# Convolution layers: the pivot subtracted by TensorE in the tap bank, sums two tiles later, GpSimd's copies issued ahead of the sigmoid

## The chip, the cores and the metric

One core of a Trainium2 chip runs the whole program in one launch. TensorE (PE; its weight loads PEld), VectorE (DVE), ScalarE (ACT), GpSimd (POOL) and SyncE (SP, which issues the loads) each run their own list of instructions in order and wait for each other by semaphores. The metric is the device time of the program in microseconds, the median of three runs.

## The reference

A transformer block of four mixers and then four layers, for 512 tokens of width 1024 in float32. Layers 0 and 3 of the four have the convolution module that is changed here:

```
def dwconv(x, w, b):
    k, c = w.shape
    y = lax.conv_general_dilated(
        x, w[:, None, :].astype(x.dtype), window_strides=(1,),
        padding=[(k // 2, k // 2)], dimension_numbers=('NWC', 'WIO', 'NWC'),
        feature_group_count=c)
    return y + b

def conv_module(h, w_in, b_in, dw_w, dw_b, ln_g, ln_b, w_out):
    a, gt = jnp.split(h @ w_in + b_in, 2, axis=-1)
    u = a * jax.nn.sigmoid(gt)
    u = dwconv(u, dw_w, dw_b)
    u = layernorm(u, ln_g, ln_b)
    return jax.nn.silu(u) @ w_out
```

The convolution has 31 taps per channel (CONV_WIDTH). The layer norm takes the mean over 1024 channels and the mean of the squared differences from it.

## The kernel before, in words

Activations lie transposed: 8 chunks of 128 channels by 512 tokens. A linear layer goes output block by output block; a block of `conv_in` has 8 weight tiles of 128 x 128. A tile (`mac`, lines 1391 to 1393) is three passes of TensorE with 512 columns: weights and activations are split into a high and a low part of type float32r (XH, XL, WH, WL; HH and HL for hidden activations), and three of the four products are added up. Weights come as float32 (RAW) 8 tiles at a time; ScalarE makes the high part (line 1642), GpSimd the low part (line 2367).

In `conv_layer` blocks 2c and 2c + 1 of `conv_in` belong to chunk c: the even one is the gate half, the odd one the value half. `evac` is called behind each block. For an even block VectorE scales it out of its bank (line 1951, the "even scaling") and ScalarE takes the sigmoid (line 1723). For an odd block VectorE scales and multiplies by the gate (line 2196), which gives u in a padded buffer PD. Then the 31 taps of the chunk are shared: the first TAPS_PE[c] go to TensorE, as float32 matmuls with diagonal matrices (line 1569), which ScalarE makes (line 1838); the next TAPS_POOL[c] are copied with their gain by ScalarE (`pool_tap`, lines 1847 and 1845) into seven staging slots in BI and added by GpSimd (line 2385); VectorE has the rest (`dve_taps`), in two halves: the first half behind the gating of its own chunk, the second behind that of the next one. VectorE's first, third, ... tap gather in one bank, its second, fourth, ... in TensorE's tap bank, so its second tap waits for TensorE's taps. Two joins (lines 2226 and 2228) add up the three parts.

For the layer norm every chunk's output has a pivot subtracted, the mean over the 128 channels of chunk 0: TensorE's `pivot` (line 1583), ScalarE's copy out of the bank (line 1857). Chunks 0 and 1 have it subtracted later (`less_pivot`, line 2246), the others in VectorE's first tap (line 2208; without a pivot lines 2205 and 2214). Then ScalarE squares a chunk (line 1671) and TensorE adds up the chunk and its square over channels in two banks (`add_up`, line 1577).

The order on each engine is that in which `walk` calls the steps. Work that isn't due yet is put in two queues: `later(fn, delay, first=True)` in `soon`, sorted by the tile at which it is due, and without `first` in `bg`; behind each tile one due step is taken, from `soon` first. PSUM has 8 banks, handed out in turn (`banks`); a bank that is taken again waits for what last freed it.

At the end of the layer VectorE finishes chunk 7 (`join_last`), its square and sums follow, `keep_warm(n)` puts n matmuls of no use on TensorE, and mean, scale and SiLU lead to the output projection `conv_out`.

Of the kernel before, what the change touches and what calls it, by code (L numbers as in the profile page):

```python
# [9 lines left out]
T = 512  # L10
# [15 lines left out]
OUT_ORDER = (4, 5, 0, 1, 2, 3, 6, 7)  # L26
TAPS_PE = (2, 3, 3, 4, 4, 4, 6, 16)
TAPS_POOL = (8, 8, 8, 8, 8, 8, 8, 7)
# [113 lines left out]
def build(nc, wst, xin, prm, cst, gatew, cmpw1, cmpw2, relm, natb, rope, dist, out):  # L142
# [7 lines left out]
    with ExitStack() as ctx:  # L150
# [81 lines left out]
        def walk(steps):  # L232
# [708 lines left out]
            def conv_layer(norm, nxt, ci, bias_free):  # L941
                cur = {}
# [5 lines left out]
                def tap(c, j):  # L948
                    return pcol("conv_dw_w", 248 * ci + 31 * c + j)
# [17 lines left out]
                def dve_taps(ch, a, b):  # L967
                    c = ch["c"]
                    j0 = TAPS_PE[c] + TAPS_POOL[c]
                    step("dve_taps", ci, c, a, b, ch["own"].ap, ch["own"].free, ch["two"].ap, ch["two"].free, ch["pe"],  # L970
                         ch["pad"].ap[:, j0:542], [tap(c, j) for j in range(j0, 31)], cur["p"].ap if c > 1 else None, cur["p_made"] if c > 1 else None,
                         ch["u"])

                def finish(ch):
# [16 lines left out]
                    if c == 0:  # L991
                        later(pivot, 13, first=True)
                        return
                    if c == 1:
                        for k in range(2):
                            o, made = outs[k]
                            outs[k] = (o, (step("less_pivot", o.ap, cur["p"].ap, made, cur["p_made"]), "o"))
                            later(lambda k=k: square(k), 13, first=True)
                            later(lambda k=k: add_up(k), 18)
                        cur["d"], cur["var"] = banks.get(), banks.get()  # L1000
                    elif c < 7:
                        later(lambda: square(c), 13, first=True)
                        later(lambda: add_up(c), 18)

                def pivot():
                    bank = banks.get()
                    cur["p"] = tiles.get()
                    i = step("pivot", cur["p"].ap, cur["p"].free, outs[0][0].ap, outs[0][1], bank.ap, bank.free)
                    bank.done((i, "p"))
                    cur["p_made"] = (i, "p")  # L1010

# [22 lines left out]
                def evac(m, bank, made):  # L1034
                    c = m // 2
                    n_pe = TAPS_PE[c]
                    if m % 2 == 0:
                        g = tiles.get()
                        z = scaled(g.ap, bank, norm, made, g.free)
                        i = step("sigmoid", g.ap, g.ap, pcol("conv_b_in", 16 * ci + 8 + c), (z,))  # L1040
                        cur["g"] = (g, (i, "sig"))
                        if c:
                            pool_taps(cur["ch"], TAPS_POOL[c - 1] // 2, TAPS_POOL[c - 1])
                        return
# [18 lines left out]
                    def pe_taps():  # L1063
                        step("pe_taps", dgs, dg_made, pad.ap, ch["u"], ch["acc"].ap, ch["acc"].free, ch["pe"])
                        for s in dg:
                            s.done(ch["pe"])
# [10 lines left out]
                step("tables")  # L1077
                keep_warm(2)
                finish(cur["ch"])
# [3 lines left out]
                keep_warm(4)  # L1083
                cur["p"].done(("tap", ci, 7, 0))
                pt_free[0] = pt_free[1] = (cur["squares"],)
# [297 lines left out]
        def tensor(e):  # L1383
# [178 lines left out]

            def pe_taps(i, dgs, dg_made, pad, u_made, bk, bk_free, event):
                for x in bk_free:
                    w.wait_ge(*at(x))
                w.wait_ge(*at(dg_made))
                w.wait_ge(*at(u_made))
                for j in range(len(dgs)):
                    t = e.matmul(bk, dgs[j], pad[:, j:j + T], start=j == 0, stop=j == len(dgs) - 1)  # L1569
                t.then_inc(*did(pe_made, event))  # L1570

            def add_up(i, first, last, d, d_free, o, o_made):
# [4 lines left out]
                e.matmul(d, ones, o, start=first, stop=last).then_inc(*did(pe_made, (i, "mm")))  # L1577

            def pivot(i, p, p_free, o, o_made, bank, bank_free):
                for event in bank_free:  # L1580
                    w.wait_ge(*at(event))
                w.wait_ge(*at(o_made))
                e.matmul(bank, ones, o, start=True, stop=True).then_inc(*did(pe_made, (i, "mm")))

# [28 lines left out]
            def ret_out(i, c, os, made, bank, bank_free, g, g_made, gain):  # L1613
# [10 lines left out]
                nat_scores=nat_scores, nat_turn=nat_turn, nat_values=nat_values, gates=gates, cmp_product=cmp_product, cmp_kv=cmp_kv, cmp_norm=cmp_norm, cmp_scores=cmp_scores,  # L1624
                cmp_turn=cmp_turn, cmp_values=cmp_values, pe_taps=pe_taps, add_up=add_up, pivot=pivot, warm=warm, ret_scores=ret_scores,
                ret_values=ret_values, ret_out=ret_out))

        def scalar(e):
# [223 lines left out]

            def pivot(i, p, p_free, o, o_made, bank, bank_free):
                for event in p_free:
                    w.wait_ge(*at(event))
# [57 lines left out]
        def vector(e):  # L1913
# [283 lines left out]

            def dve_taps(i, ci, c, a, b, own, own_free, two, two_free, pe_event, pad, taps, p, p_made, u_made):
# [407 lines left out]
```

## Time and profile before

| what | us |
|---|---|
| median of three runs | 3226.23 (3224.87 to 3229.0) |
| the profiled execution | 3229.4 |
| its span, first to last instruction | 3227.6 |
| TensorE busy in the span | 3151.7 (98%) |
| VectorE, ScalarE, GpSimd busy | 1451.8, 1255.6, 1545.0 |

The span is what the trace covers; the execution's own time is 1.8 us longer. Busy times are sums over instructions; a matmul's end is modelled, so starts are compared here rather than ends.

### The profile page before, as it was taken

What the parts mean: (1) busy time and instruction counts of PE and PEld (TensorE: products, weight loads), DVE (VectorE), ACT (ScalarE), POOL (GpSimd) and SP (SyncE); (2) the same over time, 40 slices, a digit from 0 to 9 for tenths busy, and PEclk for the clock granted to TensorE, in tenths of its full rate; (3) what the DMA queues carried; (4) which work ended last, traced back from release to release, by engine and by line L of the source; (5) the groups of instructions that cost most, each with busy time, mean ns of one, the idle gap of its engine ahead of it and who ended that gap; (6) DMA issues with size and microseconds to landing.
All of it is one profiled execution on the core that took longest, in us unless ns stands there. A gap on an engine that the chain in (4) does not pass through costs nothing. (4 is left out here: it accounts for less than half of the span.)

```text
span 3227.6 us, 34930 instructions
## 1 busy us (share of the span) xinstructions
PE 3151.7 (98%) x13893; PEld 2472.8 (77%) x13893; DVE 1451.8 (45%) x2674; ACT 1255.6 (39%) x1858; POOL 1545.0 (48%) x764
## 2 busy tenths in 40 slices
PE   8999999989999999999999999999999998999999
PEld 5668888865788887778888877787888885578887
DVE  5554111388643345446243523331624359853433
ACT  5553222255443345554343322222434344543333
POOL 3225555567354453334554533443455457545454
PEclk9999999999999999999999999999999999999999
DMA  4213333221232333222323322222232331133322
GB/s 182 76 46 92 98 92 98 92 68 56 66 99 97 98 98 102 94 86 87 103 92 98 112 70 67 72 91 68 90 104 92 98 98 53 40 92 101 95 96 88
DMA packets 80674, 286.03 MB, mean 89 GB/s; under 512 B 9088, under 2 KB 9344, under 8 KB 80384
## 3 DMA queue, kind: packets, MB, share of 16 engines
q1 hardware_dynamic: 80512, 283.80, 27.8%
q8 instruction: 110, 1.80, 0.2%
q14 instruction: 52, 0.43, 0.0%
HBM read 281.40 MB, written 2.10 MB: 88 GB/s over the span
## 5 line engine op out<-in xcount | busy, mean ns | idle before, releaser
L2367 POOL TENSOR_TENSOR WL<-RAW,WH 128x1024 fp32r<-128x1024 f32 x504 | 1216.8, 2416 | 1257.4 <-ACT WH L1642 1257.1
L1391 PE MATMUL PS<-XH,WH 128*128 128x512 f32 x2640 | 1076.4, 408 | 30.1 <-ACT TT L1857 14.0
L1393 PE MATMUL PS<-XH,WL 128*128 128x512 f32 x2640 | 1032.2, 391 | 0.0
L1392 PE MATMUL PS<-XL,WH 128*128 128x512 f32 x2640 | 1031.9, 391 | 0.0
L1642 ACT ACTIVATE WH<-RAW 128x1024 fp32r<-128x1024 f32 x504 | 529.2, 1051 | 548.1 <-PE PS L1393 458.8
L1391 PEld LDWEIGHTS PS<-XH,WH 128*128 128x128 f32 x2640 | 498.3, 189 | 171.4 <-issue 45.7
L1392 PEld LDWEIGHTS PS<-XL,WH 128*128 128x128 f32 x2640 | 498.5, 189 | 116.2 <-issue 19.0
L1393 PEld LDWEIGHTS PS<-XH,WL 128*128 128x128 f32 x2640 | 497.7, 189 | 105.8
L1391 PE MATMUL PS<-HH,WH 128*128 128x512 f32 x1264 | 495.6, 392 | 8.6 <-DVE HL L2265 4.4
L1392 PE MATMUL PS<-HL,WH 128*128 128x512 f32 x1264 | 493.5, 390 | 0.0
L1393 PE MATMUL PS<-HH,WL 128*128 128x512 f32 x1264 | 493.3, 390 | 0.0
L1946 DVE TENSOR_TENSOR X<-PS,X 128x512 f32<-128x512 f32 x168 | 115.2, 688 | 507.0 <-PE PS L1393 507.0
L2372 POOL TENSOR_TENSOR HL<-TT,HH 128x512 fp32r<-128x512 f32 x142 | 184.2, 1298 | 329.8 <-ACT HH L1646 329.6
L1951 DVE TENSOR_TENSOR PD<-PS,TT 128x512 f32<-128x512 f32 x178 | 123.3, 693 | 375.1 <-PE PS L1393 355.6
L1391 PEld LDWEIGHTS PS<-HH,WH 128*128 128x128 f32 x1264 | 238.3, 189 | 61.4 <-issue 6.1
L1393 PEld LDWEIGHTS PS<-HH,WL 128*128 128x128 f32 x1264 | 238.3, 189 | 49.8
L1392 PEld LDWEIGHTS PS<-HL,WH 128*128 128x128 f32 x1264 | 238.4, 189 | 49.4 <-issue 0.2
L1744 ACT ACTIVATE PS<-PD,PRM 128x512 f32<-128x512 f32 x176 | 137.8, 783 | 224.1 <-DVE PD L1951 223.7
L1646 ACT ACTIVATE HH<-TT 128x512 fp32r<-128x512 f32 x142 | 90.0, 634 | 340.5 <-DVE PD L1927 177.9
L2187 DVE SCALAR_TENSOR_TENSOR PS<-PD,PRM,PS 128x512 f32<-128x512 f32 x176 | 133.0, 756 | 149.9 <-ACT PS L1744 149.9
L1951 DVE TENSOR_TENSOR TT<-PS,TT 128x512 f32<-128x512 f32 x118 | 90.5, 767 | 240.2 <-PE PS L1393 222.5
L2219 DVE SCALAR_TENSOR_TENSOR PS<-PD,PRM,PS 128x512 f32<-128x512 f32 x268 | 179.1, 748 | 16.1 <-PE PS L1569 16.1
(242 smaller groups left out, 2414.5 us busy)
## 6 DMA issues: line engine op xcount, KB each, us to landing
RAW<-wst SPq DMA_DIRECT2D x504, 512.0 KB, 3.5
BI<-natb SPq DMA_DIRECT2D x16, 384.0 KB, 4.5
X<-xin SPq DMA_DIRECT2D x16, 256.0 KB, 5.0
X<-cmpw SPq DMA_DIRECT2D x1, 2048.0 KB, 9.5
out<-X SPq DMA_DIRECT2D x8, 256.0 KB, 2.0
BI<-relm SPq DMA_DIRECT2D x4, 448.0 KB, 10.4
PRM<-prm SPq DMA_DIRECT2D x1, 685.0 KB, 12.8
BI<-rope SPq DMA_DIRECT2D x2, 256.0 KB, 4.1
```

The source lines that it names most:

```text
L1391: e.matmul(o, wh, h, start=first, stop=False)
L1392: e.matmul(o, wh, l, start=False, stop=False)
L1393: t = e.matmul(o, wl, h, start=False, stop=last)
L1642: e.activation(WH[:, b % NSPLIT, :], RAW[:, b % NRAW, :], ACT.Copy).then_inc(*did(hi_made, ("hi", b)))
L1646: e.activation(HH[:, k, :], src, ACT.Copy).then_inc(*did(act_made, (i, "hi")))
L1744: e.activation(bank, pad[:, 1:513], ACT.Identity, scale=pcol("ffn_dw_w", 132 * layer + 44 + ch), bias=pcol("ffn_dw_b", 44 * layer + ch)).t ...
L1946: e.tensor_tensor(X[:, m, :], bank, X[:, m, :], ADD).then_inc(*did(dve_made, (i, "x")))
L1951: e.tensor_tensor(dst, bank, rs, MUL).then_inc(*did(dve_made, (i, "z")))
L2187: e.scalar_tensor_tensor(bank, pad[:, 0:512], pcol("ffn_dw_w", wn + ch), bank, MUL, ADD).then_inc(*did(dve_made, (i, "l")))
L2219: e.scalar_tensor_tensor(bank, pad[:, n:n + T], taps[n], bank, MUL, ADD).then_inc(*did(dve_made, ("tap", ci, c, n)))
L2367: e.tensor_tensor(WL[:, b % NSPLIT, :], RAW[:, b % NRAW, :], WH[:, b % NSPLIT, :].bitcast(f32), SUB).then_inc(*did(lo_made, ("lo", b)))
L2372: e.tensor_tensor(HL[:, k, :], src, HH[:, k, :].bitcast(f32), SUB).then_inc(*did(pool_made, (i, "lo")))
```

## The change

Five things are done in the convolution layers. (1) The pivot is no longer brought out of a bank: ScalarE writes −1/128 as a weight tile into HL and a copy of chunk 0's output into HH, both of type float32r, and TensorE multiplies the two: once into the bank of the sums (`pivot_sum`, where chunks 0 and 1 take it from, line 2241 of the new file) and once per chunk from chunk 2 on at the end of its tap matmuls. VectorE's first tap has the plain form in all chunks. The sum over chunks takes chunk 0 in. (2) Two taps of TensorE, one in chunk 4 and one in chunk 6, go to VectorE. (3) The sums are due 20 tiles behind their chunk's joins instead of 18, in the sorted queue; the banks of the sums are taken one chunk earlier. (4) The second half of a chunk's copies for GpSimd stands ahead of the next sigmoid. (5) Two of the six `keep_warm` matmuls go.

```
-TAPS_PE = (2, 3, 3, 4, 4, 4, 6, 16)
+TAPS_PE = (2, 3, 3, 4, 3, 4, 5, 16)
...
                     if c == 0:
                         later(pivot, 13, first=True)
+                        later(pivot_sum, 20, first=True)
+                        cur["d"], cur["var"] = banks.get(), banks.get()
                         return
                     if c == 1:
                         for k in range(2):
                             o, made = outs[k]
-                            outs[k] = (o, (step("less_pivot", o.ap, cur["p"].ap, made, cur["p_made"]), "o"))
+                            outs[k] = (o, (step("less_pivot", o.ap, cur["d"].ap, made, ("pivot_sum", ci)), "o"))
                             later(lambda k=k: square(k), 13, first=True)
-                            later(lambda k=k: add_up(k), 18)
-                        cur["d"], cur["var"] = banks.get(), banks.get()
+                            later(lambda k=k: add_up(k), 20, first=True)
                     elif c < 7:
                         later(lambda: square(c), 13, first=True)
-                        later(lambda: add_up(c), 18)
+                        later(lambda: add_up(c), 20, first=True)
...
                 def add_up(k):
                     o, made = outs[k]
-                    if k:
-                        i = step("add_up", k == 1, k == 7, cur["d"].ap, cur["d"].free, o.ap, made)
-                        cur["mean"] = (i, "mm")
+                    i = step("add_up", k == 0, k == 7, cur["d"].ap, (outs[0][1], outs[1][1]), o.ap, made)
+                    cur["mean"] = (i, "mm")
...
                     if m % 2 == 0:
+                        if c:
+                            pool_taps(cur["ch"], TAPS_POOL[c - 1] // 2, TAPS_POOL[c - 1])
                         g = tiles.get()
                         z = scaled(g.ap, bank, norm, made, g.free)
                         i = step("sigmoid", g.ap, g.ap, pcol("conv_b_in", 16 * ci + 8 + c), (z,))
                         cur["g"] = (g, (i, "sig"))
-                        if c:
-                            pool_taps(cur["ch"], TAPS_POOL[c - 1] // 2, TAPS_POOL[c - 1])
                         return
...
                 step("tables")
-                keep_warm(2)
                 finish(cur["ch"])
...
+            def pivot_sum(i, ci, d, d_free):
+                for event in d_free:
+                    w.wait_ge(*at(event))
+                w.wait_ge(*at(("pivot", ci)))
+                e.matmul(d, HL[:, 7, 0:128], HH[:, 7, :], start=True, stop=True).then_inc(*did(pe_made, ("pivot_sum", ci)))
+
...
                 for j in range(len(dgs)):
-                    t = e.matmul(bk, dgs[j], pad[:, j:j + T], start=j == 0, stop=j == len(dgs) - 1)
+                    t = e.matmul(bk, dgs[j], pad[:, j:j + T], start=j == 0, stop=pivot_made is None and j == len(dgs) - 1)
+                if pivot_made is not None:
+                    w.wait_ge(*at(pivot_made))
+                    t = e.matmul(bk, HL[:, 7, 0:128], HH[:, 7, :], start=False, stop=True)
...
-            def pivot(i, p, p_free, o, o_made, bank, bank_free):
-                for event in p_free:
-                    w.wait_ge(*at(event))
-                w.wait_ge(*at((i, "mm")))
-                e.activation(p, bank, ACT.Copy, scale=1.0 / 128).then_inc(*did(act_made, (i, "p")))
+            def pivot(i, event, o, o_made):
+                e.activation(HL[:, 7, 0:128], ones, ACT.Copy, scale=-1.0 / 128)
+                w.wait_ge(*at(o_made))
+                e.activation(HH[:, 7, :], o, ACT.Copy).then_inc(*did(act_made, event))
...
-                        if p is None:
-                            t = e.tensor_scalar(own, pad[:, 0:T], taps[0], None, MUL)
-                        else:
-                            w.wait_ge(*at(p_made))
-                            t = e.scalar_tensor_tensor(own, pad[:, 0:T], taps[0], p, MUL, SUB)
-                        t.then_inc(*did(dve_made, ("tap", ci, c, 0)))
+                        e.tensor_scalar(own, pad[:, 0:T], taps[0], None, MUL).then_inc(
+                            *did(dve_made, ("tap", ci, c, 0)))
...
-                e.tensor_tensor(o, o, p, SUB).then_inc(*did(dve_made, (i, "o")))
+                e.tensor_tensor(o, p, o, ADD).then_inc(*did(dve_made, (i, "o")))
```

ScalarE in chunk 1 and the start of chunk 2 of the first convolution layer, the difference in its order (WH is the weight split, line 1723 the sigmoid, lines 1847 and 1845 the copies for GpSimd):

```order
-L1723 ACTIVATE TT<-TT,PRM 128x512
-L1845 ACTIVATE BI<-PD,PRM 128x512 x4
-L1642 ACTIVATE WH<-RAW 128x1024
-L1857 ACTIVATE TT<-PS 128x512
+L1845 ACTIVATE BI<-PD,PRM 128x512 x4
+L1723 ACTIVATE TT<-TT,PRM 128x512
+L1642 ACTIVATE WH<-RAW 128x1024
+L1854 ACTIVATE HL<-CST 128x128
+L1856 ACTIVATE HH<-TT 128x512
 L1847 ACTIVATE BI<-PD,PRM 128x512
 L1845 ACTIVATE BI<-PD,PRM 128x512 x3
 L1838 ACTIVATE PT<-CST,PRM 128x128 x4
```

The sigmoid has moved behind the four copies, and two copies out of SBUF (lines 1854 and 1856 of the new file) stand where the copy out of the pivot's bank stood.

TensorE around the pivot in the same layer, before: the pivot's matmul behind the fifth tile of block 5, the rest of that block, and the first pass of block 6 (bank PS2):

```order
L1583 MATMUL PS2<-TT,CST 128x512 [waits dve_made]
L1391 MATMUL PS3<-XH,WH 128x512
L1392 MATMUL PS3<-XL,WH 128x512
L1393 MATMUL PS3<-XH,WL 128x512
L1391 MATMUL PS3<-XH,WH 128x512
L1392 MATMUL PS3<-XL,WH 128x512
L1393 MATMUL PS3<-XH,WL 128x512
L1391 MATMUL PS3<-XH,WH 128x512
L1392 MATMUL PS3<-XL,WH 128x512
L1393 MATMUL PS3<-XH,WL 128x512
L1391 MATMUL PS2<-XH,WH 128x512 [waits lo_made,act_made]
```

And now, in block 6: the fourth tile, the pivot's sum, the fifth tile, and chunk 2's taps:

```order
L1388 MATMUL PS2<-XH,WH 128x512
L1389 MATMUL PS2<-XL,WH 128x512
L1390 MATMUL PS2<-XH,WL 128x512
L1564 MATMUL PS1<-HH,HL 128x512 [waits act_made]
L1388 MATMUL PS2<-XH,WH 128x512
L1389 MATMUL PS2<-XL,WH 128x512
L1390 MATMUL PS2<-XH,WL 128x512
L1572 MATMUL PS5<-PD,PT 128x512 [waits dve_made]
L1572 MATMUL PS5<-PD,PT 128x512 x2
L1575 MATMUL PS5<-HH,HL 128x512
```

The matmul of 512 float32 columns in block 5 has gone; block 6 no longer waits for ScalarE, and a pass of HL and HH stands in block 6 and behind the taps. The first pass of block 6 is in bank PS2 as before and waits for VectorE, which scaled block 4 out of it.

TensorE at the sums of chunk 1 in block 8, before:

```order
L1577 MATMUL PS5<-TT,CST 128x512
L1577 MATMUL PS1<-TT,CST 128x512 [waits act_made]
L1391 MATMUL PS2<-XH,WH 128x512
L1392 MATMUL PS2<-XL,WH 128x512
L1393 MATMUL PS2<-XH,WL 128x512
L1391 MATMUL PS2<-XH,WH 128x512
L1392 MATMUL PS2<-XL,WH 128x512
L1393 MATMUL PS2<-XH,WL 128x512
L1569 MATMUL PS0<-PD,PT 128x512 [waits dve_made]
L1569 MATMUL PS0<-PD,PT 128x512 x3
```

And now, with those of chunk 0 (banks PS1 for the chunks, PS3 for the squares):

```order
L1583 MATMUL PS1<-TT,CST 128x512
L1583 MATMUL PS3<-TT,CST 128x512 [waits act_made]
L1388 MATMUL PS2<-XH,WH 128x512
L1389 MATMUL PS2<-XL,WH 128x512
L1390 MATMUL PS2<-XH,WL 128x512
L1583 MATMUL PS1<-TT,CST 128x512
L1583 MATMUL PS3<-TT,CST 128x512 [waits act_made]
L1388 MATMUL PS2<-XH,WH 128x512
L1389 MATMUL PS2<-XL,WH 128x512
L1390 MATMUL PS2<-XH,WL 128x512
L1572 MATMUL PS0<-PD,PT 128x512 [waits dve_made]
L1572 MATMUL PS0<-PD,PT 128x512 x3
```

The two pairs of sums stand behind the fourth and fifth tile of the block now, not around the third, and each pair has a sum of the chunk ahead of that of its square.

## Rows read from the trace of the kernel before

**Rows 1.** Busy times by stretch; columns: stretch, its length, then each engine, granted clock, DMA

```profile
666.66:821.11 154.45, 134.97 (x450) 86.18 (x449) 133.35 (x206) 79.20 (x140) 105.06 (x69) 0.96 0.16 51
...
2661.39:2814.65 153.26, 134.53 (x450) 86.14 (x448) 133.38 (x206) 79.21 (x140) 105.04 (x69) 0.96 0.16 51
```

**Rows 2.** Waits of TensorE, 640 to 840 us: total us, times, longest

```profile
PE PS L1577 <- ACT TT L1671: 7.1, 4, 3.0
...
PE PS L1391 <- ACT TT L1857: 6.9, 1, 6.9
```

**Rows 3.** TensorE in order of time: start us, us, instruction [idle before <-releaser]

```profile
698.20 0.80 PE L1391 MATMUL PS<-XH,WH 128*128 128x512 f32 x1 [6.89 <-ACT TT L1857]
...
706.07 0.40 PE L1392 MATMUL PS<-XL,WH 128*128 128x512 f32 x1
...
713.10 0.39 PE L1393 MATMUL PS<-XH,WL 128*128 128x512 f32 x1
```

**Rows 4.** ScalarE in order of time, chunks 1 to 3

```profile
693.55 0.72 ACT L1723 ACTIVATE TT<-TT,PRM 128x512 f32<-128x512 f32 x1 [9.83 <-DVE PD L1927]
...
694.18 2.54 ACT L1845 ACTIVATE BI<-PD,PRM 128x512 f32<-128x512 f32 x4
...
697.58 0.57 ACT L1857 ACTIVATE TT<-PS 128x512 f32<-128x512 f32 x1
...
718.58 1.14 ACT L1671 ACTIVATE TT<-TT 128x512 f32<-128x512 f32 x2
```

**Rows 5.** VectorE in order of time, chunks 1 to 3

```profile
692.84 0.68 DVE L1951 TENSOR_TENSOR TT<-PS,TT 128x512 f32<-128x512 f32 x1
...
694.38 0.75 DVE L2196 SCALAR_TENSOR_TENSOR PD<-PS,PRM,TT 128x512 f32<-128x512 f32 x1 [0.22 <-ACT TT L1723]
...
701.81 0.69 DVE L2226 TENSOR_TENSOR TT<-PS,BI 128x512 f32<-128x512 f32 x1
...
703.14 3.16 DVE L2246 TENSOR_TENSOR TT<-TT 128x512 f32<-128x512 f32 x2
...
707.92 6.01 DVE L2219 SCALAR_TENSOR_TENSOR PS<-PD,PRM,PS 128x512 f32<-128x512 f32 x9
...
713.85 0.67 DVE L1951 TENSOR_TENSOR TT<-PS,TT 128x512 f32<-128x512 f32 x1
...
730.63 2.07 DVE L2219 SCALAR_TENSOR_TENSOR PS<-PD,PRM,PS 128x512 f32<-128x512 f32 x3 [5.03 <-PE PS L1569]
```

**Rows 6.** Two short stretches with the granted clock (PEclk, third column from the right)

```profile
698.20:701.40 3.20, 3.20 (x8) 2.55 (x9) 3.20 (x6) 3.20 (x7) 3.06 (x3) 0.50 0.00 0
...
719.25:725.10 5.85, 5.85 (x10) 2.98 (x10) 5.73 (x9) 5.13 (x10) 5.65 (x4) 0.50 0.11 9
```

**Rows 7.** TensorE in order of time, end of the first layer

```profile
794.64 13.98 PE L1569 MATMUL PS<-PD,PT 128*128 128x512 f32 x32 [1.67 <-DVE PD L2196]
...
808.46 3.60 PE L1577 MATMUL PS<-TT,CST 128*128 128x512 f32 x8
...
813.60 1.88 PE L1577 MATMUL PS<-TT,CST 128*128 128x512 f32 x4
```

**Rows 8.** Groups of VectorE instructions by line, 655 to 821 us: busy us, mean ns

```profile
L2208 DVE SCALAR_TENSOR_TENSOR PS<-PD,PRM,TT 128x512 f32<-128x512 f32 x6 | 8.9, 1486 | 0.0
...
L2228 DVE TENSOR_TENSOR TT<-PS,TT 128x512 f32<-128x512 f32 x7 | 4.8, 692 | 0.2
...
L2246 DVE TENSOR_TENSOR TT<-TT 128x512 f32<-128x512 f32 x2 | 3.2, 1620 | 0.0
...
L2205 DVE TENSOR_SCALAR PS<-PD,PRM 128x512 f32<-128x512 f32 x2 | 1.5, 749 | 0.0
```

**Rows 9.** First weight wait of the output projection; VectorE in the second layer

```profile
835.18 0.47 PE L1391 MATMUL PS<-HH,WH 128*128 128x512 f32 x1 [1.35 <-POOL WL L2367]
...
2687.69 0.68 DVE L1951 TENSOR_TENSOR TT<-PS,TT 128x512 f32<-128x512 f32 x1
```

**Rows 10.** GpSimd in order of time, chunk 2

```profile
702.80 4.64 POOL L2385 TENSOR_TENSOR BI<-BI 128x512 f32<-128x512 f32 x3
```

More of the change, by code:

```diff
@@ L970, in dve_taps @@
                     step("dve_taps", ci, c, a, b, ch["own"].ap, ch["own"].free, ch["two"].ap, ch["two"].free, ch["pe"],
-                         ch["pad"].ap[:, j0:542], [tap(c, j) for j in range(j0, 31)], cur["p"].ap if c > 1 else None, cur["p_made"] if c > 1 else None,
-                         ch["u"])
+                         ch["pad"].ap[:, j0:542], [tap(c, j) for j in range(j0, 31)], ch["u"])
                 def finish(ch):
@@ L996, in finish, with pivot_sum @@
                             o, made = outs[k]
-                            outs[k] = (o, (step("less_pivot", o.ap, cur["p"].ap, made, cur["p_made"]), "o"))
+                            outs[k] = (o, (step("less_pivot", o.ap, cur["d"].ap, made, ("pivot_sum", ci)), "o"))
                             later(lambda k=k: square(k), 13, first=True)
-                            later(lambda k=k: add_up(k), 18)
-                        cur["d"], cur["var"] = banks.get(), banks.get()
+                            later(lambda k=k: add_up(k), 20, first=True)
                     elif c < 7:
                         later(lambda: square(c), 13, first=True)
-                        later(lambda: add_up(c), 18)
+                        later(lambda: add_up(c), 20, first=True)
                 def pivot():
[L1006 to L1010, printed above, removed]
+                    step("pivot", ("pivot", ci), outs[0][0].ap, outs[0][1])
+                def pivot_sum():
+                    step("pivot_sum", ci, cur["d"].ap, cur["d"].free)
                 def square(k):
@@ L1063, in pe_taps @@
                     def pe_taps():
-                        step("pe_taps", dgs, dg_made, pad.ap, ch["u"], ch["acc"].ap, ch["acc"].free, ch["pe"])
+                        step("pe_taps", dgs, dg_made, pad.ap, ch["u"], ch["acc"].ap, ch["acc"].free,
+                             None if c < 2 else ("pivot", ci), ch["pe"])
                         for s in dg:
@@ L1083, in conv_layer @@
                 keep_warm(4)
-                cur["p"].done(("tap", ci, 7, 0))
                 pt_free[0] = pt_free[1] = (cur["squares"],)
@@ L1577, in add_up @@
                 e.matmul(d, ones, o, start=first, stop=last).then_inc(*did(pe_made, (i, "mm")))
-            def pivot(i, p, p_free, o, o_made, bank, bank_free):
-                for event in bank_free:
-                    w.wait_ge(*at(event))
-                w.wait_ge(*at(o_made))
-                e.matmul(bank, ones, o, start=True, stop=True).then_inc(*did(pe_made, (i, "mm")))
             def warm(i, bank, free, n):
@@ L1624, in tensor @@
                 nat_scores=nat_scores, nat_turn=nat_turn, nat_values=nat_values, gates=gates, cmp_product=cmp_product, cmp_kv=cmp_kv, cmp_norm=cmp_norm, cmp_scores=cmp_scores,
-                cmp_turn=cmp_turn, cmp_values=cmp_values, pe_taps=pe_taps, add_up=add_up, pivot=pivot, warm=warm, ret_scores=ret_scores,
+                cmp_turn=cmp_turn, cmp_values=cmp_values, pe_taps=pe_taps, add_up=add_up, pivot_sum=pivot_sum, warm=warm, ret_scores=ret_scores,
                 ret_values=ret_values, ret_out=ret_out))
@@ L1851, in tables @@
                 ln_exp()
-            def pivot(i, p, p_free, o, o_made, bank, bank_free):
-                for event in p_free:
-                    w.wait_ge(*at(event))
-                w.wait_ge(*at((i, "mm")))
-                e.activation(p, bank, ACT.Copy, scale=1.0 / 128).then_inc(*did(act_made, (i, "p")))
+            def pivot(i, event, o, o_made):
+                e.activation(HL[:, 7, 0:128], ones, ACT.Copy, scale=-1.0 / 128)
+                w.wait_ge(*at(o_made))
+                e.activation(HH[:, 7, :], o, ACT.Copy).then_inc(*did(act_made, event))
             def mean_square(i, d, mean, t, t_free):
@@ L2196, in gated, with dve_taps @@
                 e.scalar_tensor_tensor(u, bank, bias, g, ADD, MUL).then_inc(*did(dve_made, (i, "u")))
-            def dve_taps(i, ci, c, a, b, own, own_free, two, two_free, pe_event, pad, taps, p, p_made, u_made):
+            def dve_taps(i, ci, c, a, b, own, own_free, two, two_free, pe_event, pad, taps, u_made):
                 for n in range(a, b):
```

2 lines of the change are left out of this document (1 added, 1 removed).

## The prediction

> **What bounds the kernel now.** I first looked for the stretches that the edits touch. The change sits in the two convolution layers only. The busy times by stretch [rows 1] take each from its first tap matmul to the first product of its output projection: 154.45 and 153.26 us, in which TensorE is busy for 134.97 and 134.53, VectorE for 133.35 and 133.38. So neither engine alone fills the stretch; they wait for each other. Outside, both layers' neighbours do not change.
>
> Then the waits of TensorE in the first of these layers [rows 2]: the longest single one, 6.9 us, ends on ScalarE's line 1857, the copy of the pivot out of its bank; four waits for squares (line 1671) make 7.1 us, the longest 3.0. The order of time shows why they are long. TensorE stops until 698.20 [rows 3], because block 6 takes the bank that the pivot's copy frees. That copy ran at 697.58, behind a sigmoid that began at 693.55 after 9.83 us of idling [rows 4], which waited for VectorE's scaling at 692.84 [rows 5]. VectorE had no gap of note there: from 694.38 to 713.85 its row is packed. So the pivot wait is at its root a VectorE backlog, and taking the pivot out of the way leaves part of it.
>
> After such waits the granted clock is 0.50 for 3.20 us behind the pivot wait and for 5.85 us behind the 3.0 us square wait [rows 6], the 1.2 GHz level of TensorE's two; TensorE's work in those stretches takes twice its time.
>
> **Unit prices.** A float32 matmul costs TensorE (808.46 − 794.64) / 16 = 0.864 us [rows 7]. A pass of a weight tile costs (713.10 − 706.07) / 31 = 0.227 [rows 3], a tile of three 0.68. On VectorE the gating multiply and ten taps take 701.81 − 694.38 = 7.43, the two joins 1.33, nine taps 713.85 − 707.92 = 5.93, so 0.659 each; from the even block's scaling to the gating multiply 694.38 − 692.84 = 1.54 [rows 5]. A first tap in the pivot form averages 1.49, in the plain form 0.75 (in a row of taps 0.66, as instructions overlap); less_pivot takes 1.62 from two SBUF tiles, and 0.69 is the row of the form with one operand in PSUM [rows 8].
>
> **The change, part by part, for one layer.** TensorE loses two tap matmuls, the pivot's matmul and two warming ones (5 × 0.864 = 4.3 us) and gains one sum, the pivot's sum and six short passes (0.864 + 7 × 0.227 = 2.5). The trace has no short pass behind float32 taps into the same bank. Its instruction has the weight tile's shape and type, so I take 0.227; the bounds are 0 and a tap's 0.864, of which four per layer turn out to be on the path (chunks 3, 5, 6, 7): between 0.9 us less and 2.5 us more per layer. VectorE loses 6 × 0.74 at the first taps and about 1.9 at less_pivot and gains two taps, 1.3: 4.9 us less. ScalarE gains one 128-column copy, bounded by 0 and the pivot copy's 0.57 [rows 4]; it lies in ScalarE's idle time, and without that it would put off the copies for GpSimd by as much.
>
> The path, station by station, in the first layer:
>
> Nothing ahead of VectorE's scaling of block 4 (692.84) is altered on VectorE, so that stays. The banks of the two sums are taken a chunk earlier, so the blocks take turns on two banks from block 4 on, and block 6 waits for the scaling of block 4 instead of the pivot's copy: TensorE goes on at 693.57, not 698.20, having idled some 4 us, and the gating of chunk 2 stays at 694.38. If the clock is then at 1.2 GHz for 3.20 us again (1.6 us lost), 16 tiles, the pivot's sum and chunk 2's taps end at 709.1.
>
> The pivot's sum needs ScalarE's copy (693.55, a sigmoid of 0.72, a weight split of 0.86, being 697.58 − 694.18 less the four copies' 2.54, and two copies: about 696) [rows 4] and TensorE gets there at 696.3 or later. VectorE wants it at 703.14; 5 us to spare. Then VectorE: two less_pivots at 0.66 give 704.45, ten taps 711.04 (before 713.85), scaling done at 711.74. TensorE waits for that, 709.1 to 711.75.
>
> From there 6 tiles, two sums of two matmuls and chunk 3's taps (4 × 0.864 + 0.227) take 11.22; with 1.6 us for a clock that a 2.6 us wait has lowered, 724.6. VectorE has been ready for its second tap since 722.0 (711.04 + 1.54 + 7.43 + 1.33 + 0.66). Before, this tap began at 730.63 after 5.03 us of waiting [rows 5]. A square is done 0.72 + 0.86 + 0.57 (1.14 for two [rows 4]) = 2.2 us behind the even scaling, since the four copies for GpSimd no longer stand in between; the sum over it comes 2.72 + 0.864 = 3.6 us behind that scaling where VectorE is the later engine, and later still where TensorE is. So the square waits go, with about 1.4 us to spare.
>
> Eight taps: 729.9. Ten tiles: TensorE at 731.4; chunk 4 gated at 732.3. VectorE 7.43 + 1.33 + 10 × 0.659 gives 747.65, done 748.35; TensorE is there at 746.8 (16 tiles 10.88, two sums 1.73, three taps and the short pass 2.82) and waits until 748.4. Chunk 5: VectorE 747.65 + 1.54 + 14.69 (7.43 + 1.33 + 5.93) = 763.9; TensorE 748.4 + 16.29 (four taps) = 764.7, now the later. Chunk 6 is gated at 765.6; TensorE takes 17.16 more (five taps): 781.85; VectorE 14.69: 780.3. Chunk 7 is gated at 782.75; the sum for chunk 5 waits for its square until 783.2 (chunk 6's scaling ends at 781.0) and ends at 784.05; sixteen taps and the short pass: 798.1, where the taps ended at 808.46 before [rows 7].
>
> VectorE gets to that point at 797.6; two more additions 799.6, square 800.2. TensorE has finished chunk 6's sums at 799.85 and does the last two with no warming matmuls ahead: 801.6. Before, the last two began at 813.60, right behind the two warming matmuls, and ended 2 × 0.864 later, 815.33 [rows 7]. That is 13.7 us earlier. The chain behind it (5.8 us to the first product at 821.11, then 14.07 to the weight block at 835.18 [rows 9]) is untouched, and the projection restarts on that weight block whatever the clock did in between.
>
> The second layer had its scaling of block 4 at 2687.69 [rows 9]. The same 114.6 us (692.84 to 821.11 − 13.7 = 807.4) end at 2802.3 instead of 2814.65 [rows 1]: 12.4. Together 26.1 us. The profiled execution took 3229.4 us (its span 3227.6 and 1.8 around it), so 3203.3; the runs' median stands 3.2 lower, at 3226.23: **3200.1**, say 3200.
>
> **The clock, weighed.** The two stretches at half clock last 3.20 and 5.85 us [rows 6]; a wait of 2.6 us is a little shorter than the 3.0 us one that did it, so the loss per layer is between 0 and 2.9 (half of 5.85), and 1.6 is my choice. With 0 the sum is 26.1 + 3.2 = 29.3 (3197), with 2.9 it is 23.5 (3203). The Trainium skill ("TensorE: Matmul & The Clock Gate", Part 1) says that half rate is the resting state and that an idle stretch brings the array back to it until it has been active again; the change makes two idle stretches of its own, so by that rule it gives some of the gain back and the time is 3200 to 3203, not 3197. The trace agrees [rows 6].
>
> **Rivals.** (a) *VectorE paces all of it.* If each of its idle gaps (154.45 − 133.35 = 21.1 us) stays, a layer gains only its 4.9 us and the two warming matmuls' 1.7: 13 us in all, 3213. For it: VectorE is packed in chunk 2 [rows 5]. Against it: its gaps ended on TensorE, whose own waits go. (b) *Squares stay late.* If the moved sums still wait about 1 us in each of five chunks per layer, 10 us are lost: 3210. For it: only 1.4 us to spare; against it: the order puts the square straight behind the split. (c) *The copies block the sigmoid; slower.* ScalarE is in order: behind a copy that waits for a staging slot from GpSimd stand the sigmoid, the split and the square, then VectorE's gating and TensorE's taps. GpSimd has to have done the earlier additions of the chunk; against it: in chunk 2 they were done at 702.80 + 4.64 = 707.44 [rows 10] and the scaling that the sigmoid needs anyway comes at 711 even in the forecast. Once the sigmoid is late by 26.1 / 14 = 1.9 us in each of the 14 even blocks behind a chunk, the gain is gone; at 3 us each it is 3200 + 42 = 3242. (d) *The clock is not lost and the passes hide:* 3197 − 2 = 3195, and with luck in the second layer 3190.
>
> **How the numbers follow.** Forecast with its clock and pass bounds, 3195 to 3208: 0.68. (a) 0.12, (b) 0.09, (c) 0.03, (d) beyond the forecast's low end 0.05; something not seen that leaves the time as it was 0.03. The range 3191 to 3212 leaves out (c), the last and about half of (a), less than 2 in 10. About 0.2%, 6.5 us, is what a measurement here can tell from no change; all but (c) and the last end below 3219.8: faster 0.94, same 0.03, slower 0.03.
>
> **What would show it.** The copy's wait gone from TensorE's list and a wait of about 4 us for VectorE ahead of block 6 in its place; one of 1 to 3 us ahead of block 8; no waits for squares but a short one ahead of chunk 7's taps; the taps of chunk 7 ending some 131.4 us behind the first tap matmul instead of 141.8; layer stretches of about 141 us. Wrong would be: long waits of VectorE for TensorE's taps as before, ScalarE waiting for GpSimd ahead of a sigmoid, or stretches above 148.

## The result and the profile after

The changed kernel takes **3199.31 us** (median of four runs, 3197.04 to 3202.2), the kernel before 3226.88 in the runs beside them (3224.87 to 3229.0): a ratio of **0.9915**, 95% interval 0.9898 to 0.9932. It is 27.6 us faster; forecast were 3200 and 26.1.

The profiled execution took 3197.04 us (span 3195.2). First the same stretches of the two layers as in [rows 1], then three stretches behind waits (columns as there; PEclk is third from the right):

```profile
665.71:805.24 139.53, 129.50 (x449) 84.74 (x448) 128.02 (x208) 79.22 (x139) 103.11 (x69) 0.99 0.17 56
...
2645.52:2785.13 139.61, 129.20 (x449) 84.84 (x448) 128.01 (x208) 79.23 (x139) 103.07 (x69) 0.99 0.17 56
...
692.63:697.00 4.37, 4.37 (x12) 3.46 (x13) 4.15 (x7) 4.37 (x8) 2.64 (x2) 0.61 0.00 0
710.71:716.00 5.29, 5.29 (x20) 3.71 (x21) 5.07 (x8) 5.29 (x9) 3.56 (x2) 1.00 0.03 9
...
2690.62:2696.00 5.38, 5.38 (x20) 3.80 (x21) 5.16 (x8) 5.38 (x9) 3.65 (x2) 1.00 0.10 10
```

The layers are 14.92 and 13.65 us shorter than in [rows 1], 28.57 together. TensorE is busy for 5.5 and 5.3 us less there, and idles 9.5 and 8.3 us less (154.45 − 134.97 = 19.48 before, 139.53 − 129.50 = 10.03 now). Between the two layers nothing moved: 2645.52 − 805.24 and 2661.39 − 821.11 are both 1840.28. The spans differ by 32.4; the other 3.8 us are 0.95 ahead of the first layer and 2.88 behind the second, where the code is the same (see "Median and profile" below).

The waits of TensorE in the first of the layers, 640 to 830 us, beside [rows 2]:

```profile
PE PS L1388 <- DVE PD L1926: 7.7, 3, 4.0
PE PS L1388 <- DVE HL L2260: 2.2, 1, 2.2
PE PS L1388 <- POOL WL L2362: 1.3, 1, 1.3
PE PS L1583 <- ACT TT L1671: 0.2, 1, 0.2
```

The wait of 6.9 us for the pivot's copy is gone, and of the 7.1 us of waits for squares 0.2 are left. The other waits ahead of the layer's end are three for VectorE. (The first product of the projection waits for HL, its weight block for WL, as before.) In order of time on TensorE (start, us, instruction, idle before):

```profile
692.63 0.58 PE L1388 MATMUL PS<-XH,WH 128*128 128x512 f32 x1 [4.04 <-DVE PD L1926]
...
697.08 0.39 PE L1564 MATMUL PS<-HH,HL 128*128 128x512 f32 x1
...
710.71 0.50 PE L1388 MATMUL PS<-XH,WH 128*128 128x512 f32 x1 [2.21 <-DVE PD L1926]
...
745.88 0.50 PE L1388 MATMUL PS<-XH,WH 128*128 128x512 f32 x1 [1.42 <-DVE PD L1926]
...
780.96 1.12 PE L1583 MATMUL PS<-TT,CST 128*128 128x512 f32 x2 [0.17 <-ACT TT L1671]
781.92 13.90 PE L1572 MATMUL PS<-PD,PT 128*128 128x512 f32 x32
795.26 0.79 PE L1575 MATMUL PS<-HH,HL 128*128 128x512 f32 x1
795.89 3.73 PE L1583 MATMUL PS<-TT,CST 128*128 128x512 f32 x8
```

These are blocks 6, 8 and 12, and chunk 7's taps with the short pass behind them. VectorE in the same order, beside [rows 5]:

```profile
691.89 0.68 DVE L1950 TENSOR_TENSOR TT<-PS,TT 128x512 f32<-128x512 f32 x1
...
693.43 0.75 DVE L2195 SCALAR_TENSOR_TENSOR PD<-PS,PRM,TT 128x512 f32<-128x512 f32 x1 [0.22 <-ACT TT L1723]
...
702.20 1.28 DVE L2241 TENSOR_TENSOR TT<-PS,TT 128x512 f32<-128x512 f32 x2
703.40 0.75 DVE L2203 TENSOR_SCALAR PS<-PD,PRM 128x512 f32<-128x512 f32 x1
704.05 6.01 DVE L2214 SCALAR_TENSOR_TENSOR PS<-PD,PRM,PS 128x512 f32<-128x512 f32 x9
709.97 0.68 DVE L1950 TENSOR_TENSOR TT<-PS,TT 128x512 f32<-128x512 f32 x1
...
722.25 5.36 DVE L2214 SCALAR_TENSOR_TENSOR PS<-PD,PRM,PS 128x512 f32<-128x512 f32 x8 [1.23 <-PE PS L1575]
```

VectorE is packed up to block 8's scaling at 709.97 as it was up to 713.85 before, but its list is shorter: two less_pivots in 1.28 us, not 3.16, a plain first tap. Its wait for chunk 3's taps fell from 5.03 to 1.23. ScalarE:

```profile
692.61 0.72 ACT L1723 ACTIVATE TT<-TT,PRM 128x512 f32<-128x512 f32 x1 [9.00 <-DVE PD L1926]
...
694.19 0.29 ACT L1854 ACTIVATE HL<-CST 128x128 fp32r<-128x128 f32 x1
694.39 0.62 ACT L1856 ACTIVATE HH<-TT 128x512 fp32r<-128x512 f32 x1
...
710.69 0.72 ACT L1723 ACTIVATE TT<-TT,PRM 128x512 f32<-128x512 f32 x1 [8.57 <-DVE PD L1926]
711.32 1.04 ACT L1642 ACTIVATE WH<-RAW 128x1024 fp32r<-128x1024 f32 x1
712.26 1.14 ACT L1671 ACTIVATE TT<-TT 128x512 f32<-128x512 f32 x2
```

The two squares start 2.29 us behind the even scaling (709.97); before, they started 4.73 us behind it (713.85 to 718.58), with four copies in between.

### The profile page after: what moved, and what is told of

It reads as the page before. It is cut to its first block and busy times, and to the rows that moved or that the text cites. A ratio compares the mean times of both kernels' runs of the same rounds, so it can differ in the third digit from the quotient of the medians.

```text
span 3195.2 us, 34928 instructions
## 1 busy us (share of the span) xinstructions
PE 3138.7 (98%) x13891; PEld 2468.7 (77%) x13891; DVE 1441.0 (45%) x2678; ACT 1255.7 (39%) x1856; POOL 1541.2 (48%) x764
## 5 line engine op out<-in xcount | busy, mean ns | idle before, releaser
L1388 PE MATMUL PS<-XH,WH 128*128 128x512 f32 x2640 | 1069.7, 405 | 29.3 <-DVE PD L1926 15.5
```

What stands on the lines that cost most here:

```text
L1388: e.matmul(o, wh, h, start=first, stop=False)
```

## The experiments

The theory was the forecast's: the copy of the pivot was only the last link of a VectorE backlog, the squares were late because four copies stood ahead of them, and two warming matmuls at the end were pure time. The first part of it did not hold as it stands (see "Block 6" below). Its rivals: that the pivot was worth more (the short pass cheap, the bank's wait all gain), that the later sums and not the copies rid TensorE of the square waits, and that the moved taps carry part of the gain. All runs in one table: median in us, the ratio, with its interval, to runs of the kernel before that were made beside each kernel (their medians lie between 3223.85 and 3226.63), and the stretches of the two layers, taken as above (before 154.45 and 153.26, after 139.53 and 139.61):

| kernel | median | ratio | stretches |
|---|---|---|---|
| pivot as before | 3205.8 | 0.9939 [0.9924, 0.9953] | 144.58, 143.18 |
| sigmoid first | 3210.51 | 0.9953 [0.9936, 0.997] | 145.79, 144.20 |
| sums at 18 tiles | 3198.73 | 0.9918 [0.9903, 0.9933] | 139.55, 141.21 |
| both of these | 3217.93 | 0.9979 [0.997, 0.9989] | 150.94, 149.42 |
| warming matmuls | 3201.56 | 0.9923 [0.9908, 0.9938] | 141.12, 141.24 |
| taps as before | 3197.55 | 0.991 [0.9895, 0.9925] | 139.17, 139.31 |
| before, wait filled | 3225.02 | 0.9998 [0.9989, 1.0007] | 151.51, 153.31 |
| no pivot | 3194.64 | 0.9903 [0.9886, 0.992] | 137.62, 137.75 |
| other taps | 3191.07 | 0.9896 [0.988, 0.9913] | 136.03, 136.15 |
| no pivot, other taps | 3187.88 | 0.9884 [0.9869, 0.9899] | 134.13, 134.20 |

**The pivot as before**, the other four edits kept. With it go back the sum over chunk 0 and the turn of the banks (those of the sums are taken one chunk later again), which no run separates from the pivot:

```
...
-                            outs[k] = (o, (step("less_pivot", o.ap, cur["d"].ap, made, ("pivot_sum", ci)), "o"))
+                            outs[k] = (o, (step("less_pivot", o.ap, cur["p"].ap, made, cur["p_made"]), "o"))
...
-                        e.tensor_scalar(own, pad[:, 0:T], taps[0], None, MUL).then_inc(
-                            *did(dve_made, ("tap", ci, c, 0)))
+                        if p is None:
+                            t = e.tensor_scalar(own, pad[:, 0:T], taps[0], None, MUL)
+                        else:
+                            w.wait_ge(*at(p_made))
+                            t = e.scalar_tensor_tensor(own, pad[:, 0:T], taps[0], p, MUL, SUB)
+                        t.then_inc(*did(dve_made, ("tap", ci, c, 0)))
...
```

> The changed kernel with the pivot as it was (its own matmul, ScalarE's copy out of a bank, VectorE's first tap and less_pivot from two SBUF tiles); the other four edits stay. Theory (stations): the copy now runs about 1.7 us behind VectorE's scaling of block 4 instead of 4.7, so block 6 starts some 2.3 us later than in the changed kernel; block 8 waits for a VectorE that is 2.7 us later, and the first taps cost some more: stretches of 142.5 to 144.5 us against 139.5, the kernel 6 to 10 us slower than the changed one, 3205 to 3209. Rival (the pivot's bank wait of 7 us was the gain): 7 us or more per layer come back, stretches of 146 or more, 3213 or more.

The layers came out 5.05 and 3.57 us longer than after's. TensorE in order of time, blocks 6 and 8 of the first layer; VectorE's scaling of block 4; and the granted clock behind both waits, in the last line behind block 8 of the second layer:

```profile
694.31 0.79 PE L1390 MATMUL PS<-XH,WH 128*128 128x512 f32 x1 [5.33 <-ACT TT L1856]
...
713.21 0.80 PE L1390 MATMUL PS<-XH,WH 128*128 128x512 f32 x1 [2.96 <-DVE PD L1926]
```

```profile
691.39 0.68 DVE L1950 TENSOR_TENSOR TT<-PS,TT 128x512 f32<-128x512 f32 x1
```

```profile
694.31:699.00 4.69, 4.69 (x11) 3.72 (x12) 4.69 (x9) 4.69 (x10) 4.45 (x3) 0.51 0.34 94
713.21:719.00 5.79, 5.79 (x13) 4.46 (x14) 5.57 (x9) 5.79 (x11) 3.93 (x3) 0.50 0.07 17
...
2699.67:2705.46 5.79, 5.79 (x18) 4.34 (x19) 5.58 (x9) 5.79 (x11) 3.92 (x3) 0.75 0.11 21
```

Block 6 starts 694.31 − 665.20 = 29.11 us behind the first tap matmul, in after 692.63 − 665.71 = 26.92: 2.2 us later, expected 2.3. Of its wait of 5.33 us, 3.1 had passed when VectorE's scaling of block 4 was done (691.39 + 0.68); the other 2.2 are ScalarE's sigmoid, split and copy behind it. Block 8 starts at 48.01 us and in the second layer at 48.10, in after at 45.00 and 45.10, in before at 47.92. These 3.0 us, VectorE's longer list, are the larger part of what the pivot is worth. The 1.5 us between the two layers are the clock's: (0.75 − 0.50) × 5.79 = 1.4 behind block 8. The theory's size held in the second layer and lies just past its upper edge in the first; the rival's 146 did not come.

**The sigmoid first again** (the copies for GpSimd behind it):

```
-                        if c:
-                            pool_taps(cur["ch"], TAPS_POOL[c - 1] // 2, TAPS_POOL[c - 1])
                         g = tiles.get()
                         z = scaled(g.ap, bank, norm, made, g.free)
                         i = step("sigmoid", g.ap, g.ap, pcol("conv_b_in", 16 * ci + 8 + c), (z,))
                         cur["g"] = (g, (i, "sig"))
+                        if c:
+                            pool_taps(cur["ch"], TAPS_POOL[c - 1] // 2, TAPS_POOL[c - 1])
```

> The changed kernel with the four copies for GpSimd behind the sigmoid again. Theory: each square is 2.55 us later, 4.75 us behind the even scaling instead of 2.2, and the sum over it comes 3.6 us behind that scaling, so TensorE waits about 1 us in blocks 8 and 12, 0.3 to 1 us in 10 and 14, and some 2.5 us ahead of chunk 7's taps: stretches of 143 to 145 us against 139.5, 3206 to 3210. Rival (the later place of the sums hides the squares by itself): stretches within 0.5 us of 139.5, about 3199.

6.3 and 4.6 us longer: the first layer a little above what I expected, the second within it. TensorE's waits list, 640 to 830 us, and the granted clock behind the square wait ahead of chunk 7's taps, first and second layer:

```profile
PE PS L1388 <- DVE PD L1926: 5.7, 3, 3.2
PE PS L1583 <- ACT TT L1671: 4.5, 4, 2.6
PE PS L1388 <- POOL WL L2362: 3.4, 2, 2.9
```

```profile
786.18:791.00 4.82, 4.82 (x8) 2.03 (x9) 4.71 (x8) 3.10 (x5) 4.68 (x4) 0.65 0.00 0
...
2773.97:2779.00 5.03, 5.03 (x12) 2.37 (x13) 4.91 (x8) 3.10 (x5) 4.89 (x4) 1.00 0.02 3
```

The waits for squares are back, 4.5 us in four chunks, and so is a wait of 0.53 us for weights early in the layer, which before had as 0.54 us and after has not (the other 2.9 us of that line lie behind the stretch). The 1.7 us between the two layers are again the clock's, (1 − 0.65) × 4.82 = 1.7.

**The sums at 18 tiles:**

```
-                        later(lambda: add_up(c), 20, first=True)
+                        later(lambda: add_up(c), 18, first=True)
```

(both places where a sum is queued)

> The changed kernel with the sums due 18 tiles behind their joins again (in the sorted queue). Theory: the square is done 2.2 us behind the even scaling and the sum over it comes 2 tiles and a matmul, 2.2 us, behind it: waits of 0 to 0.3 us, stretches of 139.5 to 140.5, about 3199 to 3201. Rival (the two tiles are what removed the square waits): 1.4 us in each of 4 blocks, stretches of 144 or more, 3208.

The first layer is after's to 0.02 us, and its square waits are no longer than after's (0.16 us in all): the two tiles are worth nothing once the copies stand ahead. The second layer is 1.6 us longer, past the expected 140.5, and one stretch shows why; block 8's wait in it is 2.25 us, just as in after's second layer (2690.62), but here the clock fell:

```profile
2691.43 0.66 PE L1388 MATMUL PS<-XH,WH 128*128 128x512 f32 x1 [2.25 <-DVE PD L1926]
```

```profile
2691.43:2697.00 5.57, 5.57 (x14) 3.63 (x15) 5.35 (x9) 5.57 (x10) 3.70 (x3) 0.69 0.10 13
```

(1 − 0.69) × 5.57 = 1.7 us. This is the loss that the forecast put behind block 8. In the five layers of the changed kernel and its variants here where block 8 waited 2.21 to 2.26 us, it came in this one alone.

**Both undone,** sigmoid first and sums at 18 tiles, the two diffs together:

> The changed kernel with both undone: copies behind the sigmoid, sums due at 18. Theory: waits of about 2.5 us in blocks 8 and 12, 1.5 to 2 in 10 and 14, 2.5 ahead of chunk 7's taps, and perhaps a lowered clock behind them: stretches of 147 to 149.5, 3214 to 3219. Rival (the two edits overlap, either alone is enough): stretches of 141 to 145.

11.4 and 9.8 us longer than after, the first layer above what I expected, and 5.2 more than with the sigmoid first alone (150.94 − 145.79). TensorE's waits for squares, first layer:

```profile
PE PS L1583 <- ACT TT L1671: 8.7, 5, 2.4
```

So the two tiles are a second cure for the same late square: worth nothing with the copies out of the way, 5.2 with them in it. For that reason the single runs of this table don't add up to the gain of the change.

**The warming matmuls back:**

```
                 step("tables")
+                keep_warm(2)
                 finish(cur["ch"])
```

> The changed kernel with the two warming matmuls ahead of chunk 7's last sums put back. Theory: they stand in the way of sums that are ready, 2 x 0.864 = 1.7 us per layer: stretches of 141.2, 3202 to 3203. Rival (they lie in a wait and hold the clock): stretches of 139.5 and no change.

1.59 and 1.63 us longer: of their 2 × 0.864 = 1.73 nearly all lies on the path.

**TensorE's taps as before:**

```
-TAPS_PE = (2, 3, 3, 4, 3, 4, 5, 16)
+TAPS_PE = (2, 3, 3, 4, 4, 4, 6, 16)
```

> The changed kernel with TensorE's taps as before (one more in chunk 4, one more in chunk 6). Theory: chunk 4 is led by VectorE, which gets its scaling 0.6 us earlier; chunk 6 is led by TensorE, which is 0.86 us later: together 0 to 0.4 us per layer, stretches of 139.5 to 140, no change that can be told. Rival (TensorE's work is the bound): 2 x 0.86 per layer, stretches of 141.2, 3202.5.

0.36 and 0.30 us shorter than after, just below what I expected. The two moved taps gave nothing: with them on TensorE its wait of 1.42 us ahead of block 12 is gone, so it has the time for the one in chunk 4.

**Before, with its pivot wait filled** by seven matmuls of no use:

```
                     dve_taps(ch, 0, (31 - n_pe - TAPS_POOL[c]) // 2)
+                    if c == 2:
+                        step("warm", ch["acc"].ap, ch["acc"].free, 7)
```

> The kernel before with seven matmuls of no use (6.0 us) put into the wait of 6.9 us for the pivot's copy, in both layers, so that TensorE is active up to block 6. Theory (stations): block 6 and 7 run at 2.4 GHz, 1.6 us faster, but block 8 waits for VectorE's scaling anyway, so stretches within 1 us of 154.5 and 153.3, the time within 0.1% of before. Rival (the clock is where the gain of the change came from): 1.6 to 3 us per layer gained, 3220 to 3223.

TensorE, blocks 6 and 8 and the first square's sum:

```profile
696.83 0.50 PE L1393 MATMUL PS<-XH,WH 128*128 128x512 f32 x1 [0.89 <-ACT TT L1859]
...
713.24 0.50 PE L1393 MATMUL PS<-XH,WH 128*128 128x512 f32 x1 [2.61 <-DVE PD L1929]
...
717.92 1.13 PE L1579 MATMUL PS<-TT,CST 128*128 128x512 f32 x2 [3.02 <-ACT TT L1673]
```

The granted clock behind that square wait:

```profile
717.92:723.77 5.85, 5.85 (x18) 3.50 (x19) 5.72 (x9) 5.13 (x10) 5.70 (x4) 1.00 0.07 9
```

The wait is filled (0.89 left of 6.89) and the clock stays up behind it, so TensorE is done with block 7 earlier; it then waits 2.61 us ahead of block 8 where it waited 1.09. Block 8 starts 47.96 us behind the first tap matmul, before 714.58 − 666.66 = 47.92. This is the plainest evidence that VectorE, not TensorE, sets the time of block 8, in this kernel as in before. The second layer is as long as before (153.31 to 153.26), as expected; the first is 2.9 us shorter, which I had not expected: half of the 5.85 us at half clock [rows 6], which did not follow the same 3.0 us wait here (1.00). The median can't be told from before's.

**No pivot at all** (what is left out stands in the expectation):

```
-                        later(pivot, 13, first=True)
-                        later(pivot_sum, 20, first=True)
...
-                             None if c < 2 else ("pivot", ci), ch["pe"])
+                             None, ch["pe"])
...
```

> The changed kernel without any pivot: neither the subtraction in chunks 0 and 1 nor the short passes; the mean of squares less the squared mean is taken of the outputs as they are, which is the same in exact arithmetic. Theory: VectorE has two instructions less (1.25 us) ahead of block 6's scaling, TensorE four short passes of 0.227 less on the path: 2 us per layer, stretches of 137.4, 3195. If a short pass costs as much as a tap (0.864): 4.7 us per layer, stretches of 134.8, 3190.

1.91 and 1.86 us shorter than after. Block 8 (not block 6, as the expectation has it) is the one behind the two instructions on VectorE:

```profile
709.46 0.50 PE L1385 MATMUL PS<-XH,WH 128*128 128x512 f32 x1 [1.51 <-DVE PD L1923]
```

It starts 709.46 − 665.65 = 43.81 us behind the first tap matmul, in after at 45.00: 1.2 us are VectorE's, and the 0.7 left are the short passes', some 0.18 for each of four. They cost about what a pass of a weight tile costs; as dear as a tap they would have made 4.7 in all. By starts in after, sixteen taps and the pass take 795.89 − 781.92 = 13.97, sixteen taps alone 13.82 [rows 7].

**Other taps on TensorE,** moved to where it waits for VectorE (chunks 1 and 2) and from where VectorE waits for it:

```
-TAPS_PE = (2, 3, 3, 4, 3, 4, 5, 16)
+TAPS_PE = (2, 5, 4, 3, 4, 4, 4, 16)
```

> The changed kernel with TensorE's taps 2, 5, 4, 3, 4, 4, 4, 16: more where TensorE waits for VectorE (chunks 1, 2 and 4), fewer where VectorE waits for TensorE (3, 5 unchanged, 6). Theory (two engines in turn, whichever is late leads): block 8 starts 2.0 us earlier, chunk 3's taps 0.86 more, chunk 4's scaling 0.6 more: 3.5 us per layer, stretches of 136, 3192. Rival (VectorE or TensorE alone paces the layer): the sums of both engines' taps are nearly as before (42 taps instead of 40 on TensorE), so nothing gained, or 1.7 us per layer lost.

136.03 and 136.15: as expected, and block 8 starts 43.02 us behind the first tap matmul, 2.0 earlier than in after. The waits list of TensorE, first layer:

```profile
PE PS L1388 <- DVE PD L1926: 3.3, 2, 1.7
PE PS L1388 <- DVE HL L2260: 2.2, 1, 2.2
PE PS L1388 <- POOL WL L2362: 1.3, 1, 1.3
PE PS L1583 <- ACT TT L1671: 1.1, 1, 1.1
```

Of after's 7.7 us of waits for VectorE's scaling 3.3 are left, two of 1.67 ahead of blocks 6 and 8; the one ahead of block 12 is gone. The square ahead of chunk 7 is late by 1.1 in turn.

**No pivot and other taps,** the two diffs together, the fastest kernel here:

> Both: no pivot at all (the same in exact arithmetic) and taps 2, 5, 4, 3, 4, 4, 4, 16. Theory: 3.5 and 2 us per layer add up where TensorE and VectorE are balanced, less where the other engine is then late: stretches of 134 to 135.5, 3188 to 3191. Rival: no better than the better of the two alone.

3187.88 us, 11.4 below the changed kernel and about 38 below before (ratio 0.9884).

## Why the prediction was right, step by step

*Block 6.* Forecast: "some 4 us" of idling for VectorE's scaling of block 4, and the gating of chunk 2 where it was. Measured 4.04 and 4.14, and the gating 693.43 − 665.71 = 27.72 us behind the first tap matmul, before 694.38 − 666.66 = 27.72. The prediction gives no sum for its 4: TensorE stopped at 698.20 − 6.89 = 691.31 there [rows 3], 2.3 us ahead of 693.57; the pivot's matmul that goes (0.86) and a weight wait that went with it (0.54) make 3.7. The clock behind it was 0.61 for 4.37 us, a loss of 1.7; forecast 1.6. **What the prediction read too simply** is the old wait, "at its root a VectorE backlog": VectorE's scaling was done at 692.84 + 0.68 = 693.52, 2.2 us into the wait, and the other 4.7 of the 6.9 us passed on ScalarE, with the sigmoid, the four copies for GpSimd, the split and the pivot's copy [rows 4]. The forecast of the time does not hang on it, as block 8 waits for VectorE in either kernel.

*VectorE's list.* From the first less_pivot to block 8's scaling it needed 709.97 − 702.20 = 7.77 us; forecast 711.04 − 703.14 = 7.90. The pivot's sum came at 697.08 (forecast 696.3 or later), without a wait. The Trainium skill ("SBUF — State Buffer", Who interferes with whom) says that a VectorE instruction with two SBUF inputs contends with a GpSimd instruction that reads SBUF. That agrees with 1.62 us each beside GpSimd's additions [rows 8, 10], and with 0.64 now with one input in PSUM. The trace of before separates the two: an addition of the same shape from two SBUF tiles at the end of its first layer, when GpSimd's last additions had ended (800.07 + 8.62 = 808.69), took 0.69 us:

```profile
800.07 8.62 POOL L2385 TENSOR_TENSOR BI<-BI 128x512 f32<-128x512 f32 x6
```

```profile
810.36 0.69 DVE L2241 TENSOR_TENSOR TT<-TT,BI 128x512 f32<-128x512 f32 x1
```

So it is GpSimd's additions beside them, and not the second SBUF input alone, that made less_pivot dear.

*Block 8.* A wait of "1 to 3 us", 2.6 by the sum: measured 2.21 and 2.25. **The term that was mis-sized** stands in the next sentence of the prediction: "with 1.6 us for a clock that a 2.6 us wait has lowered". It measured 0 in both layers of the profile (granted clock 1.00 behind the wait), and over the five layers with such a wait one loss of 1.7, 0.3 us a layer. Everything behind it is early by about that: chunk 3's second VectorE tap came 56.5 us behind the first tap matmul (forecast 724.6 − 666.66 = 57.9), block 12 80.2 (81.7), the end of chunk 7's taps 130.2 (131.4), the stretch 139.5 (140.8). With 0 for that term in both layers the working gives 29.3, the stretches measured 28.6. The forecast kept both ends, 0 and 2.9, and the run with sums at 18 tiles shows the 1.6 in one layer. I had applied the rule of the Trainium skill ("TensorE: Matmul & The Clock Gate", Part 1), that an idle stretch brings the array back to half rate, to both of the change's idle stretches. In after's trace the clock fell behind block 6's 4.04 us (0.61) and not behind block 8's 2.21 (1.00); the time that I gave for it, 3200 to 3203, was a little too high.

*Squares.* Forecast to go but for a short one ahead of chunk 7's taps: 0.17 and 0.40 us there, none elsewhere. The reason given, the copies no longer in between, is shown by the runs with the sigmoid first and with the sums at 18 tiles.

*The end.* Two warming matmuls: 1.6 us per layer of 1.7. Short passes: 0.227 each was taken; by starts in after those behind chunks 2 to 6 took 0.20 to 0.23, the one behind chunk 7 0.15.

*Median and profile.* The profiled execution is 32.4 us shorter, more than the layers give; neither of the other two parts is the change's. The 0.95 us ahead of the first layer are spread: its first tap matmul comes between 665.20 and 666.76 us in the twelve profiles. For the 2.88 behind the second: the projection's weight block starts 14.05 us (before) and 14.08 us (after) behind its first product, but in the profile of before the clock behind it was half for 6.30 us, and not in after:

```profile
2828.70:2835.00 6.30, 6.30 (x15) 4.96 (x16) 0.00 (x0) 0.00 (x0) 4.50 (x2) 0.51 0.66 177
```

```profile
2799.21:2805.50 6.29, 6.29 (x28) 5.22 (x29) 0.00 (x0) 0.50 (x1) 4.57 (x2) 1.00 0.63 185
```

That costs (1 − 0.51) × 6.30 = 3.1 us. It comes and goes over this projection in the variants of the changed kernel too, as told in the last section. The medians' 27.6 us are nearer to what the two layers gained, of which 2.9 us are the half clock in the first layer of before [rows 6] that the kernel with the filled wait did not have. By the forecast's own reckoning, 28.6 us off 3226.2 would have made 3197.7; that the median is 3199.31, within 1 us of the 3200 that has the clock term in it, is in part luck.

*Rivals.* (a) VectorE pacing all of it: its gaps in the stretch fell from 21.1 to 11.5 us. (b) Late squares: 4.5 us of waits with the copies behind the sigmoid, 0.2 with them ahead. (c) A sigmoid held up by copies: in after, all seven waits ahead of a sigmoid from 665 to 806 us ended on VectorE. (d) was right for the clock at block 8, and wrong in that the passes hide: they cost some 0.7 us of the 1.9 that a layer without any pivot is shorter.

## What to carry to other kernels

Where two engines wait for each other in turn, write down block by block which one is late, and move work there: taps moved by that list gave 3.5 us more per layer, while the change's two moved taps gave nothing. Follow a wait back past the instruction that releases it, and on to the next place where the engines meet: of the 6.9 us wait for a copy 2.2 were VectorE's and 4.7 ScalarE's list, taking the copy away left 4.0 for VectorE, and what counted was that VectorE's list up to block 8 got 3 us shorter. On an engine that works in order, put what can run early ahead of the instruction that waits; here moving two lines was worth 4.6 to 6.3 us per layer (the upper figure with 1.7 us of lowered clock in it), more than any other edit undone alone.

## What the hardware showed that I had not expected

TensorE's granted clock did not follow the length of a wait alone. Behind a wait of 3.0 us for the same square it was 0.50 for 5.85 us in the first layer of before [rows 6], and 1.00 in that of the kernel with the filled wait; behind 2.25 us ahead of block 8 it was 1.00 in after and 0.69 with the sums at 18 tiles. Where it fell, TensorE's work took about twice its time, 1.6 to 3.1 us a place. What decides it was not settled. The projections behind the 24 layers of the twelve profiles show how it comes and goes over the same code. Behind the wait of 2.2 us ahead of the first product the clock fell in 11 of them; TensorE then came later to the weight block, waited 1.25 to 1.35 us for it, and no fall followed. In the other 13 it waited 2.86 to 2.89 us there, and behind that the clock fell in 7. The first kind of fall costs nothing, as the weight block starts 14.04 to 14.08 us behind the first product in all 24; the second costs up to 3.1. Executions of one kernel spread by 1.5 to 7.5 us in these runs, and part of that can be this.

Short passes of type float32r at the end of a sum of float32 matmuls in the same bank cost no more than a pass of a weight tile (0.227 us): 0.15 to 0.23 us by the starts, and 1.9 us per layer for all that the pivot adds.
